# Hybrid layer on one core: the first stage in another order, and a reciprocal root with three steps instead of four

## What is computed

```python
h = x + mixer_block(rms_norm(x, ln1_w), ...)      # Mamba-2 SSD and gated delta rule side by side
h = h + hierarchical_moe(rms_norm(h, ln2_w), ...) # top-1 group, top-2 expert of 16, SwiGLU
return rms_norm(h, final_norm_w)

def rms_norm(x, w):
    return x * rsqrt(mean(x * x, axis=-1) + 1e-6) * w
```

## Time and profile before

| | |
|---|---|
| median of 3 runs | 916.2 us (915.78 to 919.01) |
| profiled execution, span | 916.1 us |
| PE busy | 849.8 us |
| DVE busy | 628.4 us |
| ACT busy | 492.2 us |
| POOL busy | 157.3 us |
| mean granted TensorE clock | 0.978 |
| HBM read | 168.52 MB, 185 GB/s |

### The profile page before, as it was taken

How to read it: one execution, slowest core, us unless ns; L and a number is a source line. 1 busy time by engine, 2 the same in 40 slices (tenths; PEclk the granted TensorE clock), 3 DMA queues, 4 the chain that set the end, 5 groups by cost and what they waited for, 6 DMA issues and landing times.

```text
span 916.1 us, 15309 instructions
## 1 busy us (share of the span) xinstructions
PE 849.8 (93%) x5614; PEld 770.0 (84%) x5614; DVE 628.4 (69%) x792; ACT 492.2 (54%) x543; POOL 157.3 (17%) x216
## 2 busy tenths in 40 slices
PE   4999999998999999999879989999999999999993
PEld 2999999897998989989879987778878887887882
DVE  3599888555545556363697654899589769958973
ACT  5366555445444344443872332767486657748641
POOL 0012000008836748273040000000000000000000
PEclk9899999999999999999988999999999999999997
DMA  7254555222122122212252646389699968969931
GB/s 304 76 194 151 192 190 191 109 93 92 47 97 88 46 92 71 107 51 66 97 205 92 214 174 266 139 318 357 244 328 352 364 241 313 360 243 328 351 135 46
DMA packets 24478, 169.99 MB, mean 186 GB/s; under 512 B 2688, under 2 KB 3200, under 8 KB 4480
## 3 DMA queue, kind: packets, MB, share of 16 engines
q1 hardware_dynamic: 23024, 165.69, 50.0%
q10 hardware_dynamic: 1424, 3.90, 1.1%
HBM read 168.52 MB, written 1.05 MB: 185 GB/s over the span
## 4 chain that ended last, share of the span: by engine, by line
PE 73%; DVE 14%; issue 7%; ACT 5%; DMA 1%; DVEq 0%; ACTq 0%
PE ps L1309 11%; PE ps L1311 10%; PE ps L1310 10%; PE ps L1306 8%; PE ps L1307 8%; PE ps L1308 8%; PE ps L1495 4%; PE ps L1706 2%; DVE ldec L846 2%; DVE rawlo L721 2%; DVE moe_lo L1147 2%; PE ps L1544 1%; PE ps L1744 1%; PE ps L1384 1%; DVE hres L1141 1%
## 5 line engine op out<-in xcount | busy, mean ns | idle before, releaser
L1308 PE MATMUL ps<-act_r,rawlo 128*128 128x256 f32 x576 | 161.5, 280 | 0.0
L1308 PEld LDWEIGHTS ps<-act_r,rawlo 128*128 128x128 f32 x576 | 109.2, 190 | 0.0
L721 DVE TENSOR_TENSOR rawlo<-raw,whi 128x2048 fp32r<-128x2048 f32 x34 | 82.5, 2428 | 34.3 <-ACT whi L400 34.3
L1306 PE MATMUL ps<-act_r,whi 128*128 128x256 f32 x352 | 102.5, 291 | 1.8 <-DVE act_r L731 1.8
L1307 PE MATMUL ps<-act_r,whi 128*128 128x256 f32 x352 | 99.1, 281 | 0.0
L751 DVE SCALAR_TENSOR_TENSOR cacc<-ps,prm,cacc 128x255 f32<-128x255 f32 (+1 forms) x144 | 58.3, 475 | 24.0 <-ACT cacc L431 24.0
L1306 PEld LDWEIGHTS ps<-act_r,whi 128*128 128x128 f32 x352 | 67.3, 191 | 2.6 <-DVE act_r L731 2.6
L400 ACT CAST whi<-raw 128x2048 fp32r<-128x2048 f32 x34 | 64.7, 1902 | 5.4 <-PE ps L1311 5.4
L1307 PEld LDWEIGHTS ps<-act_r,whi 128*128 128x128 f32 x352 | 67.2, 191 | 0.0
L1310 PE MATMUL ps<-rawlo,xg 128*128 128x512 f32 x160 | 63.4, 396 | 0.0
L1309 PE MATMUL ps<-whi,act_r 128*128 128x256 f32 x192 | 57.7, 301 | 0.0
(11 more groups left out here) (357 smaller groups left out, 2498.9 us busy)
## 6 DMA issues: line engine op xcount, KB each, us to landing
raw<-w_mix SPq DMA_DIRECT2D x60, 1024.0 KB, 4.8
raw<-w_gate SPq DMA_DIRECT2D x24, 1024.0 KB, 5.2
moe_raw<-w_down SPq DMA_DIRECT2D x24, 1024.0 KB, 5.1
raw<-w_up SPq DMA_DIRECT2D x16, 1024.0 KB, 5.3
moe_raw<-w_up SPq DMA_DIRECT2D x16, 1024.0 KB, 5.4
moe_raw<-w_gate SPq DMA_DIRECT2D x8, 1024.0 KB, 5.9
raw<-w_down SPq DMA_DIRECT2D x8, 1024.0 KB, 5.2
xy<-x SPq DMA_DIRECT2D x1, 1024.0 KB, 6.9
```

Of the source, the lines that this page charges most:

```text
L721: dve.tensor_tensor(los[j], raw[:, j, :], f32(his[j % slots]), ALU.subtract).then_inc(lo_done, 1)
L1306: pe.matmul(dst, w_hi, a_hi, start=start, stop=False)
L1308: return pe.matmul(dst, w_lo, a_hi, start=False, stop=stop)
```

## The change

- x is loaded as two DMAs, one for each tile of 128 tokens, each with a semaphore of its own; ACT squares each tile when it is there.
- SP's order is now: x in two parts, pieces 0 and 1, `sml`, `row`, pieces 2 and 3, masks. ACT issues only constants and parameters.
- The scaling of the tiles goes from ACT to DVE, directly behind the root.
- `rsqrt` has three steps instead of four, in all its six calls.
- PE waits in the first eight steps of piece 0 for the low part of block k alone.
- `keep_warm(3)` becomes `keep_warm(2)`, `keep_warm(4)` becomes `keep_warm(1)`.
- DVE converts the masks behind `taps(3)`, before `decays_out`; ACT waits for that before `hi` of piece 6, PE before the delta loop.

```diff
         @block.sync
         def _(sp):
-            sp.dma_start(xin, x.rearrange("b (t p) c -> p (b t) c", p=P)).then_inc(s_x, 16)
-            for p in range(RING):
+            for t in range(NT):
+                sp.dma_start(xin[:, t, :], x[0, t * P:(t + 1) * P, :]).then_inc(s_xt[t], 16)
+            for p in range(2):
                 sp.dma_start(raw[:, p, :], w_mix[p]).then_inc(landed[p], 16)
+            sp.dma_start(sml[:, :], w_small).then_inc(s_sml, 16)
+            sp.dma_start(row[:, :], rows.partition_broadcast(P)).then_inc(s_tab, 16)
+            for p in range(2, RING):
+                sp.dma_start(raw[:, p, :], w_mix[p]).then_inc(landed[p], 16)
+            sp.dma_start(mask_in, masks).then_inc(s_mask, 16)
...
             act.dma_start(prm[:, :], params).then_inc(s_cst, 16)
-            act.dma_start(sml[:, :], w_small).then_inc(s_sml, 16)
-            act.dma_start(row[:, :], rows.partition_broadcast(P)).then_inc(s_tab, 16)
-            act.dma_start(mask_in, masks).then_inc(s_tab, 16)
...
-            act.wait_ge(s_x, 16)
             for t in range(NT):
+                act.wait_ge(s_xt[t], 16)
                 act.activation(xn[:, t, :], xin[:, t, :], ACT.Square,
                                accum_out=stat[:, 0, t:t + 1]).then_inc(ss_in, 1)
-            act.wait_ge(r_in, 1)
-            act.wait_ge(ss_in, NT)
-            for t in range(NT):
-                act.activation(xn[:, t, :], xin[:, t, :], ACT.Copy,
-                               scale=stat[:, 1, t:t + 1]).then_inc(xn_done, 1)
             hi(0, 0)
...
-            act.wait_ge(cst_r, 3)
             for p in range(RING):
...
-                    act.wait_ge(s_tab, 32)
+                    act.wait_ge(s_tab, 16)
...
+            act.wait_ge(lmask_done, 1)
             with act.Fori(1, N_CONV // RING) as q:
...
-                for i in range(4):
+                for i in range(3):
...
-                    if i < 3 or last_sem is None:
+                    if i < 2 or last_sem is None:
...
             rsqrt(NT, 1.0 / D, r_in)
+            dve.wait_ge(r_in, 1)
+            for t in range(NT):
+                dve.tensor_scalar(xn[:, t, :], xin[:, t, :], stat[:, 1, t:t + 1], None, ALU.mult).then_inc(xn_done, 1)
             lo(0, 0)
...
-            dve.wait_ge(s_tab, 32)
-            dve.tensor_copy(lmask[:, :, :, :].rearrange("p a l c -> p (a l c)"),
-                            mask_in).then_inc(cst_r, 1)
...
                 if p == 1:
+                    dve.wait_ge(s_tab, 16)
                     decays_in()
+            dve.wait_ge(s_mask, 16)
+            dve.tensor_copy(lmask[:, :, :, :].rearrange("p a l c -> p (a l c)"), mask_in).then_inc(lmask_done, 1)
             decays_out()
...
-            keep_warm(3)
+            keep_warm(2)
...
                     for k in range(KC):
+                        if isinstance(p, int) and p == 0 and m == 0:
+                            pe.wait_ge(xt_lo, k + 1)
                         ins = cm_step(j, m, k, ps[:, j, m * SEQ:(m + 1) * SEQ], (act_r[:, 0, k, :], act_r[:, 1, k, :]),
...
-            keep_warm(4)
-            pe.wait_ge(xt_lo, KC)
+            keep_warm(1)
...
-            pe.wait_ge(cst_r, 3)
+            pe.wait_ge(cst_r, 2)
+            pe.wait_ge(lmask_done, 1)
```

More of the change, by code:

```diff
@@ L256, in hybrid_layer @@
         iota = cst[:, C_IOTA:C_IOTA + P]
-        s_x, s_cst, s_tab, s_out = sem("s_x"), sem("s_cst"), sem("s_tab"), sem("s_out")
+        s_xt, s_cst, s_tab, s_out = [sem(f"s_x{t}") for t in range(NT)], sem("s_cst"), sem("s_tab"), sem("s_out")
+        s_mask, lmask_done = sem("s_mask"), sem("lmask_done")
         s_sml, s_xres, s_moep, s_fin = sem("s_sml"), sem("s_xres"), sem("s_moep"), sem("s_fin")
@@ L1206, in _ @@
             pool.wait_ge(s_cst, 32)
-            pool.wait_ge(s_tab, 32)
+            pool.wait_ge(s_tab, 16)
             pool.wait_ge(dec_v, 1)
```

## The result

The changed kernel takes 914.3 us (median of 6 executions, 912.08 to 916.42), the kernel before beside it 918.56 us (6, 915.78 to 919.01): ratio 0.9953, 95% interval 0.9931 to 0.9975, so 4.3 us faster where 6.7 us had been forecast, and 914.3 us where 909.5 had been. The first thing to read is that a time is not a span.

A forecast was written before the change was run, and what follows sets the result against it. PE was taken as the bound, busy 93% of the 916.1 us span, with gains only where it does not run or not yet. Terms -6.0 (front), +1.1 (masks), -1.2 and -0.6 (roots) gave 909.5 us, range 906.3 to 913.5.

The forecast's parts named there:

- The baseline: Starting time for the sum: the profiled span, 916.1 us, taken as the median of the runs, 916.2, but for 0.1.
- Part 1: Front up to the scaled x: halved load, shorter root, scaling on VectorE; ready at 12.65 instead of 15.02, 2.4 us won.
- Part 2: From scaled x to piece 0's end: over at 22.0 instead of 28.10, 6.0 us taken as won there; bounds 21.3 and 23.5.
- the moved DMAs: Front: sml, row and masks issued on SP; the late issue is hidden behind earlier data and costs nothing.
- The small matmuls: Behind piece 0: the same 3.1 us clock loss as before, 1.7 us less or more depending on where the fall comes.
- Part 3: Mask conversion moved behind taps(3): PE idles 2.9 us before piece 6 instead of 1.81, cost 1.1 us.
- 2.9 is nearer to 1.8: Before piece 6: argument against a clock fall, since the clock stayed up after idles of 1.79 and 1.81 us.
- the clock takes part of it: Rival, chance 0.17: a clock fall at piece 6 or a longer low stretch costs 1.7 to 3.4 us, 911.2 to 912.9.
- Part 4: Three root steps in the five later calls: 1.2 us won in the back stage, 0.6 at the end.
- The sum: Whole kernel: -6.0 + 1.1 - 1.2 - 0.6 = -6.7 us, giving 909.5 us.
- Weights land late: Rival, chance 0.08: the front yields only 2.6 us because one queue carries all loads, 912.9 us.
- The clock does not rise in time: Rival, chance 0.05: with three keep_warm PE stays at 1.2 GHz through piece 0, +2.8 us, 919.0.

The follow-up runs named there:

- e1: Kernel before with only the mask conversion moved behind the third taps, ahead of decays_out: 921.59 us, ratio 1.0032 to the kernel before.
- e4: Kernel before with three root steps instead of four in all six roots, nothing else: 918.23 us, ratio 0.9983 to the kernel before.
- e8: Changed kernel with x again as one DMA, the rest of the order kept: 912.77 us in one execution.
- e5: Changed kernel once more with no edit, as yardstick for later runs: 913.58 us, ratio 0.9933 to the kernel before.
- e11: Changed kernel with small weights, rows and masks issued by ACT again, behind the parameters: 913.38 us in one execution.
- e6: Changed kernel with mask conversion ahead of the second taps and the small 48-column matmuls laid between piece 1's steps: 908.07 us, ratio 0.9879 to the kernel before.
- e9: e6 with decays_out cut in four parts, run behind taps 3 to 6: 906.68 us, ratio 0.9869 to the kernel before.
- e7: Changed kernel with PE waiting for all eight low evacuations before piece 0: 915.74 us, ratio 0.9966 to the kernel before.
- e12: Changed kernel with the scaling of the two tiles left on ScalarE: 911.65 us in one execution.
- e10: Changed kernel with three and four keep_warm as before, instead of two and one: 914.75 us, ratio 0.9967 to the kernel before.
- e3: Changed kernel with the mask conversion ahead of the second taps, in an idle stretch of VectorE: 910.27 us, ratio 0.9898 to the kernel before.
- e2: Changed kernel with three keep_warm filling PE's idle between pieces 5 and 6: 911.45 us, ratio 0.9911 to the kernel before.

## Why the prediction was wrong, step by step

- **The baseline.** The prediction set the span, 916.1, beside the median, 916.2, and took 0.1 between them. The distance is 2.0 us, so the sum had to start from 918.1; this alone moves 909.5 to 911.4, and is four tenths of the miss of 4.8. Three runs with a median of 916.2, where all later medians are 918.6 to 919.2, had hidden it.
- **Part 1, x scaled at 12.65:** it was at 12.02. Steps, engines and durations held (12 instructions at 0.195 us, 1.42 us for two scalings); the second half of x and, with it, the start of the root came 0.6 us sooner than my 8.85, since the 7.65 of before's x was itself late (6.98 to 7.21 in e1, e4 and e8). The constants were there at 7.8, not "as before" at 9.1: in halves they land at 7.4 to 7.8 in nine of ten profiled executions and at 8.4 in one, with x whole at 8.4 to 9.1 in four.
- **Part 2, piece 0 over at 22.0:** 20.7 in the first profile, 21.3 in e5, 22.5 in e11, depending on when the level rises. Both bounds of the prediction's term were right in kind: 21.3 for an early rise, 23.5 for a late one, each 0.6 to 1.0 us later than measured, as the root started 0.6 us sooner.
- **Part 2, the moved DMAs at nothing:** right (e11).
- **The small matmuls:** right. The slow stretch was 3.4, 6.8 or 10.2 us long in the twelve profiles with the block, which costs 1.7, 3.4 or 5.1 us, the "1.7 us less or more" of the prediction; e6 and e9 show its cause, the block itself.
- **Part 3, the mask copy at 1.1 us.** The conversion and the 2.9 us of idle came as worked out. The step that failed is the next one, "2.9 is nearer to 1.8", by which the clock would stay up. Of the eight profiled executions with 2.9 us of idle before piece 6 it fell in four (the first, e5, e7, e12) and stayed up in four (e1, e8, e10, e11); of four with 1.8 us it fell in one (e6; not in before, e3, e4). The rival "the clock takes part of it" had 0.17 and came in half of the executions; its price of 1.7 to 3.4 us was right, and e1 prices the whole move at 2.9 us (1.6 to 4.4) instead of 1.1.
- **Part 4, the roots elsewhere at 1.8, with the front 2.4:** measured 1.6 together (0.5 to 2.7, e4), 1.5 (1.0 to 2.1) at full speed. All three parts are in the rows of e4, and some 0.9 of their 2.4 doesn't reach the end; the step that failed here is that each saving on an engine's string reaches the end whole, and where it is lost stays open.
- **The sum, at full speed:** 6.7 forecast, 6.5 (5.8 to 7.2) measured, which is in part luck: the roots gave some 0.9 less and, by difference, the front and its order some 0.7 more. What the sum held at nothing is the clock, 1.5 us (0 to 3) over all executions, and the baseline's 2.0.
- **The rivals.** "Weights land late" is out: raw 0 was there at 9.6. "The clock does not rise in time" is out: in every profile the matmuls were at the full level by piece 0's first or second step. That e10 with more fillers isn't better says the same. Even "the clock takes part of it" ended at 912.9; with the baseline at 918.1 it would have reached 914.8.

With the baseline of 918.1, 2.9 for the mask move, 1.8 for the roots and 6.0 for the front the sum is 913.2, where 914.3 and 913.58 were measured.

The Trainium skill, TensorE: Matmul & The Clock Gate, "Part 1: The HAM clock gate", says that how many matmuls run slow at a start differs from run to run, because the monitor's window isn't tied to the kernel. The rows agree: the same 16 transposes took 1.94, 2.79 and 3.65 us in the first profile, e5 and e7. For a price behind an idle this means a chance times a cost, and not a yes or no.

## What to carry to other kernels

Where PE idles a few us in front of dense work, price the idle at its length plus the slow stretch times the chance of a fall, and look for an idle stretch of the other engine before an instruction is put into the string that PE waits for: here that one instruction's place cost 3 to 5 us beside a gain of 4.3 to 5.6 for the whole change. Compare versions by span times granted clock beside the median, over all executions and not by one product, since falls come and go from execution to execution and the product itself moved by 4.5 us between executions of one kernel. And take the distance between span and time from an execution that has both before a sum is built on it.

## What the runs showed of the hardware

- The clock fell in an idle of 2.9 us, or within 1 us behind it, in four of eight executions (in the idle in the first profile, e5 and e7, behind it in e12), and behind 1.8 us in one of four (e6), at the same place of nearly the same program. These counts are too small to tell a chance of one half from one of a quarter. A slow stretch of 6.8 us (59.6 to 66.3 in the first profile) cost 3.0 us, the shorter ones of e6 and e12 (3.4 us) some 1.5 to 1.7.
- PE busy without a gap is no protection: inside the block of 48-column matmuls, 2.6 to 5.2 us after its start, the granted clock fell to 0.50 in all twelve profiles with the block, and it stayed at 1.00 in the two (e6, e9) that had it spread out.
- A fall avoided at one place can come at the next: seven of the nine profiles without a fall at piece 6 had one in the delta loop (from 212 to 230 us on), none of the five with one had. What decides that wasn't tried, and stays open. It doesn't give everything back: the mean clock of all executions rose from 0.9747 to 0.9780 and 0.9778 where the idle was filled or shortened (e2, e3).
